# Moving the stationary operands of an expert layer 64 to 256 bytes off the phase of its weight buffers

## The chip, the core and the metric

One core of one Trainium2 chip runs the whole program in one launch. The metric is the time of one execution on the device, in microseconds. Where several runs are shown, the median stands for them.

## The reference

Two layers of a decoder trunk over 256 tokens of width 1024, all in float32. Each layer has a token mixer (windowed attention beside a state-space branch), a layer norm, a channel mixer and a gated embedding input. The channel mixer of the first layer is a dense SwiGLU of width 2816. That of the second is the part that matters here, a top-2-of-8 expert SwiGLU:

```python
logits = (hf @ router)
top_v, top_i = lax.top_k(logits, 2)
gates = jax.nn.softmax(top_v, axis=-1)
combine = sum(one_hot(top_i, 8) * gates[..., None], axis=1)
for e in range(8):                       # w_gate_up[e]: 1024 x 7168, w_down[e]: 3584 x 1024
    gate, up = split(hf @ w_gate_up[e], 2, axis=-1)
    out = out + combine[:, e:e + 1] * ((silu(gate) * up) @ w_down[e])
```

## The kernel before

**Two-part products.** A product of two float32 matrices is made of three matmuls in the fp32r format: each operand is split in a high part (the value rounded to fp32r) and a low part (the rest), and high x high, high x low and low x high are added in PSUM. `product` does this with an activation as the stationary operand (128 columns, 512 bytes of each partition) and 512 columns of weights moving (2048 bytes):

```python
pe.matmul(dst, ah, bh, start=first, stop=False, skip_group_check=True)        # line 700
pe.matmul(dst, ah, bl, start=False, stop=False, skip_group_check=True)        # line 701
return pe.matmul(dst, al, bh, start=False, stop=last, skip_group_check=True)  # line 702
```

`product_by_column` (lines 707 to 709) is the same with the weights stationary and 256 columns of an activation moving. The first operand of a matmul is the stationary one. In the names of the profile, `psum<-wh,xgh` is a matmul with wh moving and xgh stationary.

**The weight stream.** Weights come from HBM in units of 1 MiB (128 partitions x 2048 float32) through a ring of six slots (`ring`), by transfers that SyncE issues at line 596. In the expert layer ScalarE writes the high part of a unit to one of three slots of `wh` or to `wh_spare` (line 451), VectorE writes the low part to the `wl` slot of the same number (line 457) and so frees the ring slot, and TensorE takes them in order. In the layers before, low parts also go back to the ring itself under the name `ring_split`, and high parts to `hi_late`, `hi_norm` and others.

**The expert layer.** The tokens of one expert are gathered into 128 rows by a matmul with a matrix of picks. An item is one expert (a second pass is there for experts with more rows). For each item `xgh` and `xgl` hold the gathered rows, transposed, as high and low parts; gate and up (28 units) are products with xgh and xgl stationary. The hidden values, in seven chunks of 512, are turned by four transposes each (line 1154), written as `hidh` by ScalarE (line 1530) and `hidl` by VectorE (line 2149), and down (14 units) is made of products with these stationary. The result is split in `yeh` and `yel` and brought back to token order by matmuls with `spread` stationary (lines 1226 and 1227). The order of units, of gate, up and down chunks is written out by hand (`STEPS`, `AHEAD`, and `middle` and `ending` on each engine), and one TensorE instruction follows the other without regard to addresses. The dense layer uses hidh and hidl too, with wh and ring_split moving.

**Where tiles lie.** `place` puts a tile at 16512 + 4 x at bytes of every partition, `at` in float32 elements. `overlay` puts the next tile right behind the last. In before, the addresses and their remainders by 512 are:

| Tiles | address (bytes) | mod 512 |
|---|---|---|
| ring, ring_split, xbh, xbl, xIl, hi_norm | 16512 + multiples of 512 | 128 |
| xTh | 100512 | 160 |
| wh; wl; wh_spare | 125632; 167616; 109248 | 192 |
| xTl; mTh, mTl; aTh, aTl, gsh, gsl; hi_late | 117440; 200384, 208576; ... | 192 |
| xgh; xgl | 204480; 208576 | 192 |
| hidh; hidl | 150208; 154304 | 192 |
| yeh, yel, pick, spread | 212672, 117440, 216768, 219840 | 192 |

Slots and slices step by 512 bytes or more, so each tile keeps its remainder throughout.

Of the kernel before, what the change touches and what calls it, by code (L numbers as in the profile page):

```python
# [13 lines left out]
F32 = mybir.dt.float32  # L14
F32R = mybir.dt.float32r
# [6 lines left out]
P = 128  # L22
D = 1024
SEQ = 256
DEPTH = 2
KD = D // P
# [8 lines left out]
DFF, DFE, NE, PLE = 2816, 3584, 8, 256  # L35
# [53 lines left out]
def program(nc, x, xT_in, pT_in, relb, hot_in, const_in, sinks, lre_in, lim_in, ldt_in, bc_in,  # L89
# [3 lines left out]
    with ctx:  # L93
# [4 lines left out]
        def place(name, shape, dt=F32, at=None):  # L98

            n = int(np.prod(shape[1:]))  # L100
            if at is None:
                at = top[0]
                top[0] += -(-n // 8) * 8
                assert BASE + 4 * top[0] <= END, (name, top[0])
            return nc.alloc_sbuf_tensor_at(name, shape, dt, offset=BASE + 4 * at)
# [40 lines left out]
        mTh, mTl = (place(n, [P, KD, SEQ], F32R, at=arena_at + SHIFTED_AT + i * KD * SEQ) for i, n in enumerate(("mTh", "mTl")))  # L146
        over = [arena_at]

        def overlay(name, shape, dt=F32):
            t = place(name, shape, dt, at=over[0])  # L150
            over[0] += int(np.prod(shape[1:]))
            assert BASE + 4 * over[0] <= END, name
            return t

        xTl = overlay("xTl", [P, KD, SEQ], F32R)
        wh = overlay("wh", [P, SPLIT, UNIT], F32R)
        wl = place("wl", [P, SPLIT + 1, UNIT], F32R, at=arena_at + PROD_AT)
        wh_spare = place("wh_spare", [P, UNIT], F32R, at=bias_at)
        hidh_at = over[0]
        hidh = overlay("hidh", [P, 2, 512], F32R)  # L160
        hidl = overlay("hidl", [P, 2, 512], F32R)
        pTh = place("pTh", [P, 2, SEQ], F32R, at=hidh_at)
        pTl = place("pTl", [P, 2, SEQ], F32R, at=arena_at + RAW_AT)
        pth_at = over[0]
# [7 lines left out]
        assert over[0] <= arena_at + PROD_AT  # L172
        over = [arena_at + LATE_AT]
        hid = overlay("hid", [P, 2, 512])
        xgh = overlay("xgh", [P, KD, P], F32R)
        xgl = overlay("xgl", [P, KD, P], F32R)
        yeh = overlay("yeh", [P, D], F32R)
        yel = place("yel", [P, D], F32R, at=arena_at)
        pick = overlay("pick", [P, 2, 2 * P], F32R)
        pickw = overlay("pickw", [P, 2, P])  # L180
        spread = overlay("spread", [P, 2, P], F32R)
        slotw = overlay("slotw", [P, 2, P])
        rl = overlay("rl", [NE, SEQ])
        topi = overlay("topi", [P, NB, 8], U32)
        assert over[0] <= arena_at + RAW_AT - 480
        rt = pT[:, 0, 0:KD * 8].rearrange("p (a b) -> p a b", a=KD)
# [5 lines left out]
        at = [0]  # L192
# [2141 lines left out]
```

## Time and profile before

| | |
|---|---|
| three runs | 1614.34, 1614.43, 1617.41 us; median 1614.43 |
| profiled execution | span 1611.1 us from the first to the last instruction |
| span beside the median | 3.3 us less, for start and end outside the span |
| TensorE matmul, weight load, VectorE, ScalarE busy | 97%, 83%, 84%, 61% of the span |
| read from HBM | 453.01 MB |
| granted TensorE clock, mean | 0.995 |

The span is that of one profiled execution, and the durations used further on come from it. Busy shares are means over stages that differ: the first 600 us or so are mixers and the dense layer, the rest is the expert layer. Matmuls overlap with their neighbours, so the distance from start to start says how fast TensorE gets through them, and not the duration column.

### The profile page before, as it was taken

To read this page: it belongs to the slowest core of one execution; us is meant where nothing else is said; L and a number is where in the kernel's file an instruction comes from. 1 tells how busy PE (TensorE), PEld (TensorE's weight loads), DVE (VectorE), ACT (ScalarE), POOL (GpSimd) and SP (SyncE) were. 2 spreads that over 40 slices of the span, in tenths; PEclk is the share of its full clock that TensorE was granted. 3 is DMA by queue.
4 is the path that set the end of the run, shared out by engine and by line. 5 is a ranking of instruction groups with operands and counts; after the bars stand their busy time and mean duration, and the time that the engine had idled before them with its cause. 6 is when DMAs were issued, how large, how long until landed. Compare 5 with 4: busy or idle time off the path is not lost.

```text
span 1611.1 us, 23897 instructions
## 1 busy us (share of the span) xinstructions
PE 1568.9 (97%) x8952; PEld 1332.2 (83%) x8952; DVE 1356.8 (84%) x1316; ACT 975.2 (61%) x887; POOL 160.5 (10%) x151
## 2 busy tenths in 40 slices
PE   7999999999999999999999999999999999999996
PEld 5889789999899978888888888888888888888884
DVE  8976866655688788999998999998999998999998
ACT  3324444434655437776777777677777777767763
POOL 5000139950300000000000000000000000000000
PEclk9999999999999999999999999999999999999998
DMA  7434855554343557999999999999999999999993
GB/s 254 157 106 137 291 193 185 190 193 137 123 139 133 209 216 294 365 364 364 367 364 334 351 370 366 356 366 342 344 367 362 363 372 333 353 371 364 350 366 121
DMA packets 168710, 456.52 MB, mean 283 GB/s; under 512 B 7926, under 2 KB 60183, under 8 KB 168136
## 3 DMA queue, kind: packets, MB, share of 16 engines
q1 hardware_dynamic: 167880, 450.91, 77.2%
q0 software_dynamic: 768, 4.75, 0.8%
q8 instruction: 43, 0.70, 0.2%
q14 instruction: 19, 0.16, 0.0%
HBM read 453.01 MB, written 2.62 MB: 283 GB/s over the span
## 4 chain that ended last, share of the span: by engine, by line
PE 85%; DVE 9%; issue 3%; DMA 2%; ACT 1%; DVEq 0%; SPq 0%; ACTq 0%
PE psum L700 20%; PE psum L701 19%; PE psum L702 19%; PE psum L707 5%; PE psum L708 5%; PE psum L709 5%; PE psum L796 5%; DVE wl L457 2%; PE psum L1154 1%; DMA ring<-in_w_out 1%; PE psum L821 1%; PE psum L769 1%; DVE hid L2144 1%; DMA ring<-in_w_in 1%; DVE small L1750 1%
## 5 line engine op out<-in xcount | busy, mean ns | idle before, releaser
L457 DVE TENSOR_TENSOR wl<-ring,wh 128x2048 fp32r<-128x2048 f32 x269 | 609.6, 2289 | 66.6 <-ACT wh L451 63.0
L451 ACT ACTIVATE wh<-ring 128x2048 fp32r<-128x2048 f32 x307 | 581.4, 1918 | 124.7 <-PE psum L702 76.8
L701 PE MATMUL psum<-wl,xgh 128*128 128x512 f32 x896 | 349.0, 390 | 0.0
L700 PE MATMUL psum<-wh,xgh 128*128 128x512 f32 x704 | 282.0, 401 | 1.0 <-DVE xgl L2128 0.5
L702 PE MATMUL psum<-wh,xgl 128*128 128x512 f32 x704 | 274.9, 390 | 0.0
L701 PEld LDWEIGHTS psum<-wl,xgh 128*128 128x128 f32 x896 | 168.5, 188 | 32.3
L700 PE MATMUL psum<-wh,hidh 128*128 128x512 f32 x440 | 172.7, 393 | 3.7 <-DVE wl L457 2.9
L701 PE MATMUL psum<-wl,hidh 128*128 128x512 f32 x448 | 174.4, 389 | 0.0
L702 PE MATMUL psum<-wh,hidl 128*128 128x512 f32 x440 | 171.4, 389 | 0.0
L457 DVE TENSOR_TENSOR wl<-ring,wh_spare 128x2048 fp32r<-128x2048 f32 x72 | 164.7, 2287 | 3.0 <-ACT wh_spare L451 3.0
L700 PEld LDWEIGHTS psum<-wh,xgh 128*128 128x128 f32 x704 | 132.2, 188 | 33.8 <-DVE wl L457 5.7
L709 PE MATMUL psum<-xTh,ring_split 128*128 128x256 f32 x560 | 157.3, 281 | 0.0
L702 PEld LDWEIGHTS psum<-wh,xgl 128*128 128x128 f32 x704 | 132.1, 188 | 28.8
L451 ACT ACTIVATE wh_spare<-ring 128x2048 fp32r<-128x2048 f32 x72 | 138.0, 1916 | 6.3 <-PE psum L702 6.3
L457 DVE TENSOR_TENSOR ring_split<-ring,wh 128x2048 fp32r<-128x2048 f32 x38 | 92.1, 2429 | 54.4 <-ACT wh L451 54.2
L1530 ACT ACTIVATE hidh<-psum 128x512 fp32r<-128x512 f32 x56 | 33.6, 600 | 162.2 <-PE psum L1154 162.2
L1599 POOL DMA_DIRECT2D lnp<-in_ln x4 | 2.4, 596 | 1258.0 <-DVEq L2180 1014.1
L709 PEld LDWEIGHTS psum<-xTh,ring_split 128*128 128x128 f32 x560 | 106.3, 190 | 0.0
L796 PE MATMUL psum<-xT,ring 128*128 128x256 f32 x416 | 94.0, 385 | 11.5 <-DMA ring<-in_w_in 11.5
L700 PEld LDWEIGHTS psum<-wh,hidh 128*128 128x128 f32 x440 | 82.6, 188 | 24.7 <-DVE wl L457 5.0
L707 PE MATMUL psum<-xTh,wh 128*128 128x256 f32 x352 | 99.4, 283 | 0.0
L796 PEld LDWEIGHTS psum<-xT,ring 128*128 128x128 f32 x416 | 79.2, 193 | 24.0 <-issue 13.2
(410 smaller groups left out, 2720.4 us busy)
## 6 DMA issues: line engine op xcount, KB each, us to landing
ring<-in_moe_gu SPq DMA_DIRECT2D x224, 1024.0 KB, 7.0
ring<-in_moe_dn SPq DMA_DIRECT2D x112, 1024.0 KB, 7.1
ring<-in_w_in SPq DMA_DIRECT2D x26, 1024.0 KB, 5.2
ring<-in_w_gu SPq DMA_DIRECT2D x22, 1024.0 KB, 5.0
ring<-in_w_dn SPq DMA_DIRECT2D x11, 1024.0 KB, 4.8
ring<-in_w_out SPq DMA_DIRECT2D x8, 1024.0 KB, 6.4
ring<-in_w_pg SPq DMA_DIRECT2D x8, 1024.0 KB, 4.9
ring<-in_w_ba SPq DMA_DIRECT2D x4, 1024.0 KB, 5.1
```

The lines of the kernel that those rows point to most:

```text
L451: eng.activation(parts(u)[0], ring[:, ring_slot(u), :], ACT.Copy).then_inc(hi_ready, 1)
L457: eng.tensor_tensor(lo, ring[:, ring_slot(u), :], hi.bitcast(F32), ALU.subtract).then_inc(lo_ready, 1)
L700: pe.matmul(dst, ah, bh, start=first, stop=False, skip_group_check=True)
L701: pe.matmul(dst, ah, bl, start=False, stop=False, skip_group_check=True)
L702: return pe.matmul(dst, al, bh, start=False, stop=last, skip_group_check=True)
L707: pe.matmul(dst, ah, bh, start=first, stop=False, skip_group_check=True)
L708: pe.matmul(dst, ah, bl, start=False, stop=False, skip_group_check=True)
L709: return pe.matmul(dst, al, bh, start=False, stop=last, skip_group_check=True)
L769: mm = pe.matmul(ps[:, d * 2 * P:(d + 1) * 2 * P], part[:, b, dc * P:(dc + 1) * P], pick[:, b, :], start=(b == 0 and part is xbh), stop=(b ...
L796: mm = pe.matmul(dst, w[:, k, t * P:(t + 1) * P], xT[:, k, :], start=(k == 0), stop=(k == KD - 1))
L821: mm = pe.matmul(bank[2 + ri][:, i * NC:(i + 1) * NC], gin[:, 8 * b + i, ri, :], u4[:, :, CL - 1], start=True, stop=True)
L1530: act.activation(hidh[:, i % 2, :], slot_group(y, e, p)[:, :], ACT.Copy).then_inc(hT_ready, 1)
```

## The change

The rows and hidden values are moved a little against the weight buffers. `overlay` can now leave elements out ahead of a tile, and four calls use it:

```diff
-        def overlay(name, shape, dt=F32):
+        def overlay(name, shape, dt=F32, skip=0):
+            over[0] += skip
             t = place(name, shape, dt, at=over[0])
             over[0] += int(np.prod(shape[1:]))
...
-        hidh_at = over[0]
-        hidh = overlay("hidh", [P, 2, 512], F32R)
-        hidl = overlay("hidl", [P, 2, 512], F32R)
+        hidh_at = over[0] + 32
+        hidh = overlay("hidh", [P, 2, 512], F32R, skip=32)
+        hidl = overlay("hidl", [P, 2, 512], F32R, skip=32)
...
         hid = overlay("hid", [P, 2, 512])
-        xgh = overlay("xgh", [P, KD, P], F32R)
-        xgl = overlay("xgl", [P, KD, P], F32R)
+        xgh = overlay("xgh", [P, KD, P], F32R, skip=16)
+        xgl = overlay("xgl", [P, KD, P], F32R, skip=32)
         yeh = overlay("yeh", [P, D], F32R)
...
         spread = overlay("spread", [P, 2, P], F32R)
+        rl = place("rl", [NE, SEQ], at=over[0])
         slotw = overlay("slotw", [P, 2, P])
-        rl = overlay("rl", [NE, SEQ])
```

After it xgh lies 64 bytes behind the phase of wh, wl and wh_spare (remainder 256 by 512), xgl 192 (384), hidh 128 (320) and hidl 256 (448). What follows them is carried along: hth, hga, hff and hgate by 256 bytes, yeh, pick, pickw, spread and slotw by 192. pTh, which shares the place of hidh, moves by 128. To make room, rl, the router's logits, now shares the place of slotw. No instruction is added, removed or reordered.

## Rows read from the trace of the kernel before

**Rows 1.** The page: TensorE's busy time, and slices of the span

```profile
PE 1568.9 (97%) x8952; PEld 1332.2 (83%) x8952; DVE 1356.8 (84%) x1316; ACT 975.2 (61%) x887; POOL 160.5 (10%) x151
...
PE   7999999999999999999999999999999999999996
...
DMA  7434855554343557999999999999999999999993
```

**Rows 2.** Windows: the expert layer's middle (six items), then all of it

```profile
core 0: us, PE busy (x) PEld busy (x) DVE busy (x) ACT busy (x) POOL busy (x), PEclk, DMA share, GB/s
756.50:1495.60 739.10, 736.73 (x3349) 603.33 (x3349) 674.87 (x451) 536.93 (x403) 0.00 (x0) 1.00 0.97 358
...
612.90:1595.60 982.70, 977.12 (x4425) 798.71 (x4423) 899.89 (x598) 710.05 (x527) 0.59 (x1) 1.00 0.95 352
```

**Rows 3.** The page's chain that ended last, by engine and line

```profile
PE 85%; DVE 9%; issue 3%; DMA 2%; ACT 1%; DVEq 0%; SPq 0%; ACTq 0%
PE psum L700 20%; PE psum L701 19%; PE psum L702 19%; PE psum L707 5%; PE psum L708 5%; PE psum L709 5%; PE psum L796 5%; DVE wl L457 2%; PE psum L1154 1%; DMA ring<-in_w_out 1%; PE psum L821 1%; PE psum L769 1%; DVE hid L2144 1%; DMA ring<-in_w_in 1%; DVE small L1750 1%
```

**Rows 4.** Waits, expert layer: weight loads, matmuls, SyncE (us, times, longest)

```profile
PEld psum L700 <- DVE wl L457: 12.5, 29, 1.3
...
PE psum L700 <- DVE wl L457: 3.4, 9, 0.9
...
SPq L596 <- DVE wl L457: 760.5, 329, 5.9
```

**Rows 5.** Tiles xgh, hidh, expert layer: one matmul of each product; turned chunks

```profile
L701 PE MATMUL psum<-wl,xgh x896: 387/389/402, 613.1 to 1581.5; 128*128 128x512 f32 x180
...
L701 PE MATMUL psum<-wl,hidh x448: 387/389/402, 648.3 to 1595.3; 128*128 128x512 f32 x150
...
L1530 ACT ACTIVATE hidh<-psum x56: 597/600/603, 641.0 to 1585.6; 128x512 fp32r<-128x512 f32 x56
L2149 DVE TENSOR_TENSOR hidl<-psum,hidh x56: 680/690/693, 644.7 to 1588.2; 128x512 fp32r<-128x512 f32 x56
```

**Rows 6.** Timeline: a matmul, and the next one's load (start us, us)

```profile
1013.15 0.39 PE L700 MATMUL psum<-wh_spare,xgh 128*128 128x512 f32 x1
1013.15 0.19 PEld L701 LDWEIGHTS psum<-wl,xgh 128*128 128x128 f32 x1
...
1013.38 0.39 PE L701 MATMUL psum<-wl,xgh 128*128 128x512 f32 x1
```

**Rows 7.** Timeline, TensorE, gate: first and last of 46 matmuls

```profile
618.38 0.39 PE L700 MATMUL psum<-wh,xgh 128*128 128x512 f32 x1
...
628.58 0.39 PE L700 MATMUL psum<-wh,xgh 128*128 128x512 f32 x1
```

**Rows 8.** Timeline, TensorE, gate: after a stop, the second to the fourteenth matmul

```profile
629.30 0.50 PE L700 MATMUL psum<-wh,xgh 128*128 128x512 f32 x1
629.64 0.40 PE L701 MATMUL psum<-wl,xgh 128*128 128x512 f32 x1
...
632.40 0.39 PE L701 MATMUL psum<-wl,xgh 128*128 128x512 f32 x1
```

**Rows 9.** Timeline, TensorE, output projection: first and last of 31 matmuls

```profile
560.08 0.40 PE L700 MATMUL psum<-ring_split,mTh 128*128 128x512 f32 x1
...
567.08 0.40 PE L700 MATMUL psum<-ring_split,mTh 128*128 128x512 f32 x1
```

**Rows 10.** Timeline, TensorE, embedding gate: first and last of 25 matmuls

```profile
595.59 0.40 PE L700 MATMUL psum<-wh,xTh 128*128 128x512 f32 x1
...
601.19 0.40 PE L700 MATMUL psum<-wh,xTh 128*128 128x512 f32 x1
```

**Rows 11.** Timeline, TensorE, dense down: first and last of 10 matmuls

```profile
266.16 0.39 PE L700 MATMUL psum<-wh,hidh 128*128 128x512 f32 x1
...
268.22 0.39 PE L700 MATMUL psum<-wh,hidh 128*128 128x512 f32 x1
```

**Rows 12.** Timeline, TensorE, branch products: twice the first and last of 10 matmuls

```profile
529.38 0.28 PE L707 MATMUL psum<-aTh,hi_late 128*128 128x256 f32 x1
...
530.44 0.28 PE L707 MATMUL psum<-aTh,hi_late 128*128 128x256 f32 x1
...
533.26 0.28 PE L707 MATMUL psum<-gsh,ring_split 128*128 128x256 f32 x1
...
534.28 0.28 PE L707 MATMUL psum<-gsh,ring_split 128*128 128x256 f32 x1
```

## The prediction

> **What bounds the kernel now.** I read the page first. TensorE is busy for 97% of the span and the slices show it full from the second one on; DMA is near full only from slice 15 on [rows 1]. Those late slices are the expert layer. Between the first expert matmul and the last, 982.7 us of 1611.1, TensorE is busy 977.1 us, VectorE 899.9, ScalarE 710.1, and the DMA engines 95% [rows 2]. The chain that ended last is 85% TensorE, and lines 700 to 702, the three matmuls of one product, are most of it [rows 3].
>
> Next the waits, since DMA at 95% could be the true bound. It isn't: no wait of TensorE or ScalarE in this stage is put down to a DMA. The queue that issues the weight loads waits 760 us for VectorE to free a ring slot [rows 4]: the transfers follow the engines. What TensorE waits for is VectorE's low part of a weight unit; its loads idled 12.5 us in 29 places for it, the matmuls themselves 3.4 us [rows 4]. So the expert layer lasts as long as TensorE takes from matmul to matmul, plus these stops. There are 896 products of three matmuls in gate and up (2688 matmuls), 448 in down (1344), and 56 turned hidden chunks [rows 5]. The granted clock is 1.00 here [rows 2], the higher level, 2.4 GHz, so the clock isn't the question.
>
> The change moves addresses and nothing else, so all hangs on whether the pace of those 4032 matmuls depends on addresses. The duration columns can't tell, since neighbours overlap; the distance between starts can. The load for one matmul starts together with the matmul before it [rows 6]: while one operand streams from SBUF, the next stationary operand is read from SBUF too. Two reads at a time, with a fixed distance between their addresses.
>
> **The pace against that distance, in before.** All distances are stationary minus moving, by the addresses of the table.
> - Distance 0, gate and up: 45 steps from 618.38 to 628.58 us, 0.2267 us each [rows 7]. Down has the same pace once it runs.
> - After any stop, same tiles: the first step takes 0.34, and the next 12 take 2.76 us, 0.040 more than at 0.2267; then it is back [rows 8]. The pace finds its way into a state in which the reads don't disturb each other.
> - Distance +64 (mTh, mTl against the ring): 30 steps in 7.00 us, 0.2333 each, for as long as the stage lasts [rows 9]. It doesn't settle.
> - Distance -32 and 0 in turn (xTh, xTl against wh and wl): 24 steps in 5.60 us, 0.2333 [rows 10].
> - Distance 0 and +64 in turn (dense down: wh and ring_split): 9 steps in 2.06 us, 0.2289 [rows 11].
> - With 256 columns moving and the weights stationary, it is the other way round: aTh against hi_late, mostly distance 0, 0.1178 a step; gsh against the ring, distance -64, 0.1133 [rows 12]. Twice 0.1133 is 0.2267: the expert layer already runs at the best pace per column that any of these stages reaches.
>
> **The change, part by part.**
> - *xgh, xgl (gate and up).* xgh goes to +64, the distance of rows 9, and xgl to +192, which is -64 in steps of 256. Two loads of three are xgh. Steps within a tile are 512 bytes for the stationary slices and 2048 for the moving ones, and the pace at distance 0 holds through all of them, so a distance repeats after 512 bytes at most. I price these matmuls at 0.2333: 2688 x 0.0066 = 17.7 us. Below: if +64 is only bad against tiles that start where the ring does, they settle at 0.2267 as now, 0 us. Above: nothing in rows 9 to 11 is slower than 0.2333.
> - *What is paid already.* After each of about 85 restarts (56 turned chunks and 29 waits) the slow steps are there now, 0.040 us each: 3.4 us, of which some 3 lie in gate and up. With a pace that never settles they aren't paid twice: -3. Were they to vanish altogether and nothing else to happen, 3.4 us would be the gain.
> - *hidh, hidl (down).* hidh goes to +128, hidl to +256. No row shows either distance for 512 columns. If what matters repeats every 128 bytes, both are distance 0 and cost 0. At the mixed pace of rows 11 it is 1344 x 0.0022 = 3.0 us, at that of rows 9, 1344 x 0.0066 = 8.9 us. I take 0: with ring and mTh swapped for weights and xgh, rows 9 say that two tiles 64 apart disturb each other, and two such steps are again the same parity. I keep 8.9 for the range.
> - *What the stops absorb.* TensorE stops when VectorE's chain of low parts is late. VectorE does a fixed amount of work ahead of each; if TensorE needs 2.9% longer for the 3 or so microseconds of units it still has ready, it arrives some 0.09 us later and waits that much less. 29 places: -2.6 us. Bounds: 0, and the 15.9 us of rows 4.
> - *The rest of the layer.* yeh, yel, spread (64 matmuls of 512 columns, lines 1226 and 1227) get one pair 64 apart, at most 64 x 0.0066 = 0.4 us. pick moves onto the phase of xbh and xbl; these 128 matmuls of 256 columns can move by 0.0045 each (rows 12), 0.6 us either way. Dense down (11 units of 24) trades +64 against +128 or -64 distances: 264 x 0.0044, 1.2 us either way. Together I take +0.4.
> - *rl over slotw*: slotw is first written in the expert layer, long after the router's logits were turned out of rl, so no wait arises: 0. Nothing is reordered; no wait is added. ScalarE's and VectorE's writes keep their shapes; in the trace hidh and hidl take 600 and 690 ns whatever TensorE reads beside them: 0.
> - *DMA.* A slower TensorE asks for less of it: 0.
>
> Sum: 17.7 - 3 + 0 - 2.6 + 0.4 = 12.5 us. The profiled execution has a span of 1611.1 us, 3.3 below the median of the runs, 1614.4; start and end around the span aren't touched. 1614.4 + 12.5 = 1626.9, so 1627.
>
> The Trainium skill speaks against any effect. its page "SBUF — State Buffer", section "SBUF: two separate sides", says that TensorE, ScalarE and VectorE's own ports never wait on anyone, and its section "Who interferes with whom" gives TensorE two independent read ports, one for the moving operand and one for weight loads. By it the pace would be one for all tiles and the sum 0, 1614.4 us. Rows 7, 9 and 10 don't agree: one shape, one clock, 0.2267 against 0.2333.
>
> **The rivals.**
> 1. *Slower in gate and up alone* (the forecast): 1627, its own range 1621 to 1632. Chance 0.60.
> 2. *Down is hit as well*: +8.9 less 1 for restarts, 1634 to 1636. For it: +128 was never measured. Against: the parity argument. Chance 0.12.
> 3. *No change.* The pace settles at 0.2267 at any multiple of 64, and rows 9 are slow because of something else in that stage (the ring's alignment; two tiles of the ring read in turn), rows 10 because of the odd 32 bytes. For it: gsh against hi_norm and the ring keeps the best pace of all at -64 [rows 12]. Or VectorE's lateness swallows most of it. 1612.5 to 1617. Chance 0.19. By the rule of the Trainium skill quoted above the time would be this one too.
> 4. *Faster.* The distance in rows 12 is the mechanism: same phase there cost 4% and 64 bytes off cured it. If in gate and up too the new distance clears the slow steps after each restart (3.4 us) with part of the 0.34 first step (85 x 0.11 = 9 us, most of it refilling), 1604 to 1611. If even 0.2267 was a disturbed pace, more would come, until the DMA decides: it moved 358 GB/s at 97% in the middle of the layer [rows 2], so 3% of 983 us, 29 us, is the most, 1585. It beats the others from the point where the steady step falls below 0.2267. Against it: no stage with single-precision products shows a step under that per column, and only restarts are left to win. Chance 0.09.
>
> **How the numbers follow.** About 0.2%, 3.2 us, is what a measurement of this kernel can tell from no change. Slower by more: cases 1 and 2 and a little of 3, 0.74; faster: case 4, 0.08; the rest 0.18. The range holds case 1, most of 3 and 2: 1612 to 1635.
>
> **What the profile after would show.** The start-to-start step in gate and up: 0.2333 and not settling (right), 0.2267 (case 3), less (case 4). The step in down: 0.2267 (right), 0.2289 or 0.2333 (case 2). Waits of weight loads for VectorE's low parts: fewer than 12.5 us if they absorb anything. VectorE's busy time unchanged, its share lower. DMA throughput below 358 GB/s in the middle of the layer. I'm wrong if the distance acts together with the absolute phase of the moving tile, or if the pace at +192 differs from that at +64, for then two thirds or one third of the 17.7 us falls away.

## The result and the profile after

The changed kernel is slower: 1628.72 us median (1627.55 to 1631.21, 4 runs) beside 1615.24 us for the kernel before (1614.34 to 1617.41, 4 runs), ratio 1.0082 with a 95% interval of 1.007 to 1.0094. The forecast was 1627. The time came out as forecast, and its parts did not: three terms were mis-sized and their errors, -3.8, +8.0 and -3.5 us, nearly cancelled. That the sum fits is luck; that the pace depends on the addresses is not.

The page of the changed kernel answers to [rows 1] and [rows 3]: the span is 1627.1 us instead of 1611.1, TensorE's busy time is 19 us longer, VectorE's the same to 2 us, and the chain leans on TensorE more (90% against 85%). A line was added ahead of them, so lines 700 to 702 are 701 to 703 here.

```profile
PE 1588.0 (98%) x8952; PEld 1336.1 (82%) x8952; DVE 1358.4 (83%) x1316; ACT 975.2 (60%) x887; POOL 158.3 (10%) x151
...
PE 90%; DVE 5%; issue 2%; DMA 1%; ACT 1%; SPq 0%; ACTq 0%; DVEq 0%
```

Windows of the changed kernel over the same two stretches of work as [rows 2] (length, then busy time and count of each engine, granted clock, DMA share, GB/s):

```profile
760.10:1509.00 748.90, 748.37 (x3351) 604.40 (x3350) 675.58 (x451) 537.04 (x403) 0.00 (x0) 1.00 0.96 353
616.50:1611.60 995.10, 992.01 (x4425) 799.64 (x4423) 900.59 (x598) 709.91 (x527) 0.59 (x1) 1.00 0.95 348
```

The expert layer takes 995.1 us instead of 982.7, with the same instructions, the same granted clock and the same busy time of VectorE and ScalarE to 0.7 us. DMA carries 353 GB/s in the middle instead of 358: it follows. So the 12.4 us are TensorE's alone. The other 3.6 us of the span's 16.0 lie ahead of the layer; the section on the prediction takes them apart.

The timeline of TensorE in the changed kernel, gate and then down, is to be read by the distance from start to start, as [rows 7]:

```profile
616.48 0.40 PE L701 MATMUL psum<-wh_spare,xgh 128*128 128x512 f32 x1
...
626.23 0.39 PE L701 MATMUL psum<-wh,xgh 128*128 128x512 f32 x1
...
902.16 0.40 PE L702 MATMUL psum<-wl,hidh 128*128 128x512 f32 x1
...
906.13 0.39 PE L701 MATMUL psum<-wh,hidh 128*128 128x512 f32 x1
```

The first pair is 42 steps apart: 9.75 us, 0.2321 each, where before had 0.2267. The second is 17 steps apart: 3.97 us, 0.2335. Neither comes back to 0.2267: the single steps repeat a pattern, 0.225 to 0.238 us in the first stretch, 0.232 to 0.235 in the second.

Weight loads wait for VectorE less than in [rows 4], where it was 12.5 us in 29 places (changed kernel, expert layer; us, times, longest):

```profile
PEld psum L701 <- DVE wl L458: 7.3, 25, 1.3
```

### The profile page after: what moved, and what is told of

Read it like the earlier page. It is cut to its first block, busy times and chain, and to the rows that moved or that the text cites. A ratio compares the mean times of both kernels' runs of the same rounds, so it can differ in the third digit from the quotient of the medians.

```text
span 1627.1 us, 23897 instructions
## 1 busy us (share of the span) xinstructions
PE 1588.0 (98%) x8952; PEld 1336.1 (82%) x8952; DVE 1358.4 (83%) x1316; ACT 975.2 (60%) x887; POOL 158.3 (10%) x151
## 4 chain that ended last, share of the span: by engine, by line
PE 90%; DVE 5%; issue 2%; DMA 1%; ACT 1%; SPq 0%; ACTq 0%; DVEq 0%
PE psum L701 21%; PE psum L703 21%; PE psum L702 21%; PE psum L708 5%; PE psum L709 5%; PE psum L710 5%; PE psum L797 5%; PE psum L1155 1%; DVE wl L458 1%; PE psum L822 1%; PE psum L770 1%; DMA ring<-in_w_out 1%; ACT wh L452 1%; DVE small L1751 1%; DMA ring<-in_w_in 1%
## 5 line engine op out<-in xcount | busy, mean ns | idle before, releaser
L703 PE MATMUL psum<-wh,xgl 128*128 128x512 f32 x704 | 279.0, 396 | 0.0
L797 PE MATMUL psum<-xT,ring 128*128 128x256 f32 x416 | 95.0, 388 | 10.9 <-DMA ring<-in_w_in 10.9
L702 PEld LDWEIGHTS psum<-wl,hidh 128*128 128x128 f32 x448 | 84.3, 188 | 20.1
```

The costliest lines, as they stand in the source:

```text
L797: mm = pe.matmul(dst, w[:, k, t * P:(t + 1) * P], xT[:, k, :], start=(k == 0), stop=(k == KD - 1))
```

## The experiments

Ten kernels were run. In each only addresses differ from one of the two kernels, through the `skip` of `overlay` or a constant; `over[0] += n` or a skip ahead of yeh brings what follows back to its phase, and rl shares the place of slotw wherever the rows are moved. The table has the mean step of all start-to-start distances up to 0.245 us in the expert layer (longer ones are restarts or stops and are left out), taken from the starts in the timeline. A step counts for the tile of its first matmul. Distances are stationary minus moving, in bytes, modulo 256.

| kernel | rows hi, lo | gate, up step (us) | hidden hi, lo | down step (us) | ratio to before (95%) |
|---|---|---|---|---|---|
| before | 0, 0 | 0.2279 | 0, 0 | 0.2270 | 1 |
| changed | 64, 192 | 0.2319 | 128, 0 | 0.2329 | 1.0082 (1.007 to 1.0094) |
| e1 | 64, 192 | 0.2320 | 0, 0 | 0.2276 | 1.0038 (1.0024 to 1.0052) |
| e2 | 0, 0 | 0.2280 | 128, 0 | 0.2335 | 1.0038 (1.0025 to 1.005) |
| e3 | 256 = 0, 0 | 0.2279 | 256 = 0, 0 | 0.2271 | 0.9999 (0.9989 to 1.0009) |
| e4 | 128, 128 | 0.2327 | 64, 64 | 0.2333 | 1.007 (1.0049 to 1.0091) |
| e5 | 32, 32 | 0.2331 | 192, 192 | 0.2294 | 1.0082 (1.0065 to 1.01) |
| e9 | 224, 224 | 0.2333 | 160, 160 | 0.2333 | 1.0093 (1.0064 to 1.0122) |
| e10 | 0, 64 | 0.2309 | 32, 32 | 0.2333 | 1.0064 (1.0041 to 1.0086) |

**e1, the rows alone.** In the changed kernel `hidh_at = over[0]` and no skip ahead of hidh and hidl:

```diff
-        hidh = overlay("hidh", [P, 2, 512], F32R, skip=32)
-        hidl = overlay("hidl", [P, 2, 512], F32R, skip=32)
+        hidh = overlay("hidh", [P, 2, 512], F32R, skip=0)
+        hidl = overlay("hidl", [P, 2, 512], F32R, skip=0)
...
-        yeh = overlay("yeh", [P, D], F32R)
+        yeh = overlay("yeh", [P, D], F32R, skip=16)
```

> Only xgh (+64 bytes) and xgl (+192) are moved; hidh and hidl stay at distance 0. Theory (each tile's own distance sets its pace, terms add up): gate and up as in the changed kernel, 0.2319 us a step against 0.2279 before, 2688 x 0.0041 = 11 us; down stays at 0.2270. Stops absorb 3 to 4 us: +7 us to +8 us over before. Rival A (the pace of down in the changed kernel was carried over from gate and up): down is slow here too, 0.2329, and the whole +13 us is here. Rival B (only the hidden tiles matter): no change.

Measured: 1622.63 us (7 runs) beside 1616.06 of before (19 runs, shared by e1 to e4), ratio 1.0038, 6.1 us. Gate and up have the step of the changed kernel, 0.2320; down is all but as before, 0.2276. Rivals A and B fall. The weight loads' waits for VectorE come to 9.6 us in 29 places.

**e2, the hidden values alone.** The other half: `skip=0` ahead of xgh and xgl, 32 ahead of hidh and hidl.

```diff
-        xgh = overlay("xgh", [P, KD, P], F32R, skip=16)
-        xgl = overlay("xgl", [P, KD, P], F32R, skip=32)
+        xgh = overlay("xgh", [P, KD, P], F32R, skip=0)
+        xgl = overlay("xgl", [P, KD, P], F32R, skip=0)
```

> Only hidh (+128 bytes) and hidl (+256) are moved. Theory: down at 0.2329 us a step against 0.2270, 1344 x 0.0059 = 8 us, gate and up unchanged at 0.2279; dense down adds about 1 us; stops absorb 2 to 3: +6 us over before. Rival A (carried over): down stays at 0.2270 and the time is that of before. Rival B: most of the +13 us.

Measured: 1622.54 us, ratio 1.0038, 6.1 us. Down is at 0.2335, gate and up at 0.2280. The two halves add up to 12.2 us beside the 13.3 that 1.0082 stands for, within the intervals: each half has its own effect, whatever the other does. A third of the products costs as much as the other two thirds, since each of its steps is worse (+0.0065 here, +0.0041 in e1).

**e3, everything 256 bytes off.**

```diff
+        hidh_at = over[0] + 64
+        hidh = overlay("hidh", [P, 2, 512], F32R, skip=64)
+        hidl = overlay("hidl", [P, 2, 512], F32R, skip=0)
...
+        xgh = overlay("xgh", [P, KD, P], F32R, skip=64)
+        xgl = overlay("xgl", [P, KD, P], F32R, skip=0)
```

> xgh, xgl, hidh and hidl all 256 bytes off. Theory (what counts repeats after 256 bytes): the same as before in every pace, 0.2279 and 0.2270, and the time within 0.2% of before. Rival (it repeats after 512 bytes only, so that 256 is as far off as can be): paces near 0.232 in both, +12 us or more.

Measured: 1615.39 us (10 runs), ratio 0.9999. TensorE's timeline of e3 in gate has 29 steps in 6.57 us between these, 0.2266 each:

```profile
621.14 0.39 PE L701 MATMUL psum<-wh,xgh 128*128 128x512 f32 x1
...
627.71 0.39 PE L703 MATMUL psum<-wh,xgl 128*128 128x512 f32 x1
```

So that tiles were moved, that rl shares a place and that hth and the rest shifted costs nothing; the distance modulo 256 does.

**e4, 128 for the rows and 64 for the hidden values.**

```diff
+        hidh_at = over[0] + 16
+        hidh = overlay("hidh", [P, 2, 512], F32R, skip=16)
+        hidl = overlay("hidl", [P, 2, 512], F32R, skip=0)
+        over[0] += 48                              # ahead of hth
...
+        xgh = overlay("xgh", [P, KD, P], F32R, skip=32)
+        xgl = overlay("xgl", [P, KD, P], F32R, skip=0)
+        yeh = overlay("yeh", [P, D], F32R, skip=32)
```

> xgh and xgl both 128 bytes off, hidh and hidl both 64. Theory (128 is a distance of its own, since down in the changed kernel was slow with two loads of three at 128): gate and up at 0.233, down at 0.233 too, like the output projection at 64: +13 us to +16 us over before. Rival (what counts repeats after 128 bytes, as the prediction took it): gate and up at 0.2279 as before, down at 0.233: +6 us.

Measured: 1628.26 us (4 runs), ratio 1.007. TensorE's timeline of e4, gate and down (a further line was added here, so the products are lines 702 to 704):

```profile
621.10 0.40 PE L702 MATMUL psum<-wh,xgh 128*128 128x512 f32 x1
...
630.86 0.40 PE L702 MATMUL psum<-wh,xgh 128*128 128x512 f32 x1
...
901.27 0.39 PE L702 MATMUL psum<-wh,hidh 128*128 128x512 f32 x1
...
904.54 0.39 PE L704 MATMUL psum<-wh,hidl 128*128 128x512 f32 x1
```

42 steps in 9.76 us, 0.2324 each at distance 128; 14 in 3.27 us, 0.2336 each at 64, the pace of the output projection at the same distance [rows 9]. The rival, that 128 is as good as 0, falls, and with it the prediction's argument by parity.

**e5, 32 and 192.** Skips of 8 ahead of xgh, 48 ahead of hidh, 0 ahead of xgl and hidl, 56 ahead of yeh and 16 ahead of hth:

```diff
+        hidh = overlay("hidh", [P, 2, 512], F32R, skip=48)
+        xgh = overlay("xgh", [P, KD, P], F32R, skip=8)
```

> xgh and xgl 32 bytes off, hidh and hidl both 192, which is -64 in steps of 256. Theory (any distance but a multiple of 256 keeps the two reads from settling): gate and up near 0.232, down near 0.233 us a step, +12 us over before, as at 64 and 128. Rival (a pace that falls with the size of the distance): gate and up at about 0.230 at 32 bytes; or -64 is free for moving 512 columns as it is for 256: down at 0.2267.

Measured: 1629.65 us (2 runs), ratio 1.0082. At 32 bytes gate and up are at 0.2331: a small distance costs the full price. Down at -64 is milder than at any other distance off 0, 0.2294; in its timeline 19 steps take 4.35 us, 0.2289 each:

```profile
902.57 0.39 PE L702 MATMUL psum<-wh,hidh 128*128 128x512 f32 x1
...
906.92 0.39 PE L703 MATMUL psum<-wl,hidh 128*128 128x512 f32 x1
```

Against the expectation, then, the sign of the distance counts.

**e9 and e10, the rest of the circle.** In e9 skips of 56 ahead of xgh and 40 ahead of hidh; in e10 none ahead of xgh, 16 ahead of xgl, 8 ahead of hidh, each with its make-up:

```diff
+        hidh = overlay("hidh", [P, 2, 512], F32R, skip=40)      # e9; e10: 8
+        xgh = overlay("xgh", [P, KD, P], F32R, skip=56)         # e9; e10: 0
+        xgl = overlay("xgl", [P, KD, P], F32R, skip=0)          # e9; e10: 16
```

> xgh and xgl both 224 bytes off (-32 in steps of 256), hidh and hidl both 160 (-96). Theory A (behind the moving tile costs less than ahead of it: -64 gave 0.2294 us a step in down where +64 gave 0.2333): gate and up between 0.2279 and 0.230, down near 0.230: +3 us to +8 us over before. Theory B (only -64 is mild): both near 0.233, +13 us.

Measured: 1631.19 us (2 runs), ratio 1.0093. Both paces are at 0.2333. Theory A falls: it isn't that lying behind is mild, -64 alone is.

> xgh on the phase of the weights, xgl 64 bytes off; hidh and hidl both 32. Theory A (each load costs by its own distance, and only then): one load of three off in gate and up, so a third of the way from 0.2279 to 0.2327, about 0.2295; down at 0.233 as gate and up were at 32: +3 us in gate and up and +8 us in down, less what stops absorb. Theory B (one load off unsettles the other two as well): gate and up at 0.232 or more, +14 us in all.

Measured: 1628.22 us (3 runs), ratio 1.0064. Gate and up are at 0.2309, between the two theories. By kind of step, from one matmul's stationary tile to the next one's: xgl to xgh 0.2340, xgh to xgh and xgh to xgl 0.2294 each. The load for a matmul runs during the matmul before it [rows 6], so xgl, the tile that is off, is loaded in the step from xgh to xgl, and that isn't the slow one. The slow one comes behind it: there xgh is loaded, on the phase, while the matmul with xgl runs. So a step isn't set by the distance of its own load alone, against theory A; what passes the delay on isn't shown.

**e6, e7 and e8, the other way: aligning the stages that are off.** The kernel before, with xTh moved onto the phase of wh (e6), with mTh and mTl moved onto that of the ring (e7), and both (e8):

```diff
+        top[0] += 8                                 # ahead of xT; += 56 ahead of bias
...
-        mTh, mTl = (place(n, [P, KD, SEQ], F32R, at=arena_at + SHIFTED_AT + i * KD * SEQ) ...
+        mTh, mTl = (place(n, [P, KD, SEQ], F32R, at=arena_at + SHIFTED_AT + 48 + i * KD * SEQ) ...
```

> The kernel before with xTh moved by 32 bytes onto the phase of wh and wl; nothing of the expert layer is moved against another. Theory: the embedding gate of the second layer (96 matmuls, distance -32 and 0 in turn, 0.2326 us a step) settles at 0.2267: -0.6 us. In the products by column, xTh then lies 64 bytes off the ring and on the phase of wh; by the branch products (0.1133 at -64, 0.1196 at 0) the second layer's input projection, now 0.1173, may lose 0.004 in each of its high-part steps, 2 us in all, and dense gate and up stay as they are: 0 to -3 us. Rival (only 512 columns depend on it): -0.6 us, within 0.2% of before.

Measured: 1617.05 us (10 runs) beside 1616.21 (29 runs, shared by e5 to e8), ratio 1.0006 (0.9997 to 1.0015). The embedding gate of the second layer does settle, which [rows 10] did not: TensorE's timeline of e6 has 14 steps in 3.18 us, 0.2271 each:

```profile
598.58 0.39 PE L702 MATMUL psum<-wh,xTh 128*128 128x512 f32 x1
...
601.76 0.39 PE L704 MATMUL psum<-wh,xTl 128*128 128x512 f32 x1
```

The gain in the products by column missed: in the second layer's input projection the mean step with the ring stationary went from 0.1180 to 0.1195 (496 matmuls, 0.7 us), in dense gate and up from 0.1159 to 0.1173 there (352, 0.5 us) and from 0.1186 to 0.1180 with wh (704, 0.4 us won). What the gate won, 96 steps from 0.2330 to 0.2281 or 0.5 us, went there.

> The kernel before with mTh and mTl moved by 192 bytes onto the phase of the ring. Theory: the output projections of both layers (192 matmuls, 0.2323 us a step at distance 64) settle at 0.2267, but for the unit whose high part is in hi_late: -0.9 us, within 0.2% of before, seen in the steps alone. Rival (the ring itself makes a stage slow, whatever the distance): 0.2323 stays.

Measured: 1616.49 us (10 runs), ratio 1.0004 (0.9994 to 1.0014). In the output projection of the second layer 16 steps take 3.63 us, 0.2269 each, where [rows 9] had 0.2333:

```profile
563.22 0.39 PE L700 MATMUL psum<-ring_split,mTh 128*128 128x512 f32 x1
...
566.85 0.39 PE L701 MATMUL psum<-ring_split,mTh 128*128 128x512 f32 x1
```

Theory right, rival wrong. The mean over both layers' 192 matmuls went from 0.2323 to 0.229, since units in hi_late are off and each change of place needs a dozen steps to settle: 0.6 us, too little to be seen in the time.

> e6 and e7 together. Theory: their terms add up, -1.5 to -4 us against before (0.1% to 0.25%); the expert layer's steps stay at 0.2279 and 0.2270. Rival: what the earlier stages gain is given back as waits for transfers or for VectorE, and the time is that of before.

Measured: 1616.43 us (12 runs), ratio 1.0000 (0.9992 to 1.0009). The steps are those of e6 and e7, and no time is won that can be measured. None of the ten kernels beats the kernel before.

## Why the prediction was right in sum and wrong in its parts

*What bounds the layer*: right. TensorE's pace sets it, and VectorE, ScalarE and DMA follow.

*The pace depends on the distance*: right, and now shown by e1 to e3: same instructions, same clock, only the distance modulo 256 differs, and the time with it. The six traces with distance 0 or 256 in gate and up lie within 0.2278 to 0.2280, the other six within 0.2309 to 0.2333, so this isn't one execution's chance. Nor is it TensorE against VectorE's or ScalarE's accesses: in the changed kernel's gate and up the 733 steps in which ScalarE did nothing average 0.2317 us and the 1689 in which it was busy throughout 0.2320; for VectorE it is 0.2320 in 247 idle steps and 0.2319 in 2135 busy ones. (DMA is busy for 95% of the layer and can't be split off in this way.) The Trainium skill's rule ("SBUF — State Buffer", section "SBUF: two separate sides"), by which TensorE never waits on anyone at its SBUF ports, and the two independent read ports of its section "Who interferes with whom", do not cover this: here the pace of matmuls with their weight loads changes by 2 to 3% with the addresses of the two operands. That the two reads disturb each other in SBUF is an inference. What is shown is the dependence on their addresses, and that neither the work of VectorE and ScalarE nor the moved tiles as such make it.

*xgh and xgl, 17.7 us less 3 for restarts that are slow already, 14.7*: the mechanism held, the size was too large. 2688 steps at 0.2319 instead of 0.2279 are 10.9 us by the unrounded means. The prediction priced xgl, at +192, like xgh, at +64, and had named just this as a way to be wrong. By the loads that run in them [rows 6], the steps of the changed kernel come out so: with a load of xgl (xgh to xgl) 0.2294, the pace that e5 found in down at 192; with a load of xgh 0.2313 (xgh to xgh) and 0.2354 (xgl to xgh), 0.2333 in the mean, as forecast. That accounts for the size. It is no law for single steps, as e10 shows, and down of the changed kernel too, where the step in which hidl is loaded, at distance 0, takes 0.2324.

*hidh and hidl, taken as 0*: wrong, the step of the prediction that failed. 1344 steps at 0.2329 instead of 0.2270 are 8.0 us by the unrounded means, near the upper bound of 8.9. The argument that two tiles 128 apart are at the same parity had no row behind it; e4 measured 128 as 0.2327. What counts repeats after 256 bytes, not 128. So it was the second rival's mechanism that came, at the first one's time.

*What stops absorb, 2.6 us*: too small. Leaving steps up to 0.245 us out, what restarts and stops cost beyond 0.2266 a step fell from 12.9 to 8.6 us in gate and up and from 5.9 to 4.1 in down, 6.1 us together, of which the waits of weight loads show 5.2 (12.5 to 7.3). The two halves alone absorb 3.3 (e1) and 3.5 us (e2). Probably a slower TensorE gives VectorE time over the whole stretch between stops, not only over the last three microseconds; no run tests that. Sum: 10.9 + 8.0 - 6.1 = 12.8, beside 12.4 between the windows.

*The rest*: +0.4 was expected. Within the layer the products with spread take 0.3 us more and those with picks 0.1 less, as small as forecast. Ahead of it, the first expert matmul comes 3.6 us later (616.5 instead of 612.9). Of this 0.45 is there by the 150th matmul, where no moved tile is in use; 0.7 comes in the first layer's branch products, which ran at the same addresses as before and yet slower (last section), and 0.3 right behind them. Another 1.0 comes in dense down, whose hidh steps went from 0.2309 to 0.2333 and hidl steps from 0.2290 to 0.2336 over 264 matmuls (0.8 us): that part is the change's, inside the 1.2 us either way of the prediction. The last 1.1 is the clock. At the start of the second layer's input projection, behind a stop of 1.57 us for VectorE, TensorE's granted clock was at its lower level, 1.2 GHz, for 15 matmuls in before and for 27 in the changed kernel, 0.2135 us a step instead of some 0.118. The windows, before and then changed (columns as in [rows 2]):

```profile
420.70:424.10 3.40, 3.36 (x15) 3.36 (x16) 3.40 (x2) 0.95 (x1) 0.00 (x0) 0.50 0.00 0
...
423.10:428.90 5.80, 5.76 (x27) 5.76 (x28) 4.39 (x2) 0.95 (x1) 0.00 (x0) 0.50 0.00 0
```

e3, with the same stop, was at 1.00 there. The profiled executions of e3 and e2 reach the first expert matmul at 613.6 and 618.0 us, so such differences come with the execution, and only the 0.8 us of dense down can be put down to the change.

*The rival "faster"*: it rested on [rows 12], where 64 bytes off beat the same phase. The last section shows that 0.1133 is only one of two paces at that distance, the other being 0.1178, so those rows didn't prove what they were taken for. In 512-column products no distance beat 0, of seven that were tried.

## What to carry to other kernels

When matmuls follow each other without a gap, measure the distance from start to start, not the duration: a difference of 2 to 3% between stages of one shape and one clock is worth a look at the tiles' addresses. For products with 128 stationary and 512 moving fp32r columns, put both operands at the same address modulo 256; a move of a tile by any other amount, made for whatever reason, can cost what it did here, 0.8% of the kernel. And when a forecast comes out right, check its terms: here one alone was off by 8 us.

## What the runs showed of the hardware that was not expected

**The pace has a memory.** At the same addresses a run of matmuls can settle into either of two paces and keep it. In the first layer's branch products, with 256 columns of gsh moving, the kernel before and e3 have the same tiles at the same places. TensorE's timelines, each with 79 steps from one row to the next; before first:

```profile
158.15 0.28 PE L707 MATMUL psum<-gsh,hi_norm 128*128 128x256 f32 x1
...
167.10 0.28 PE L708 MATMUL psum<-gsl,hi_norm 128*128 128x256 f32 x1
```

Then e3, whose lines are one further on:

```profile
158.85 0.28 PE L708 MATMUL psum<-gsh,hi_norm 128*128 128x256 f32 x1
...
168.16 0.28 PE L709 MATMUL psum<-gsl,hi_norm 128*128 128x256 f32 x1
```

8.95 us against 9.31: 0.1133 a step and 0.1178. In that stretch seven kernels (before, e1, e2, e4, e5, e8, e10) run at 0.1133 and five (changed, e3, e6, e7, e9) at 0.1178, and in none of them are these tiles moved against each other. Each had a short stop some 7 us earlier, of 0.20 us from start to start (151.16 to 151.37 in before, 151.70 to 151.90 in e3), and came out of it at one pace or the other. What decides isn't shown: the stop is 0.20 us in the changed kernel too (151.81 to 152.02).

**The price of a distance is not a slope.** 32, 64, 128, 160 and 224 bytes cost about the same, 0.2327 to 0.2333 a step; 192 costs less (0.2294), and 0 and 256 nothing (0.2270 or 0.2279 with their restarts). Why 192 is milder was not tried further.
